# Score and key products of 64 rows, issued in alternating pairs of row halves

## The reference

```
s = jnp.einsum('bqhmd,bkhmd->bhmqk', qblk, k).astype(jnp.float32) * scale
p = jax.nn.softmax(s, axis=-1)
a = p[:, :, 0] - lam * p[:, :, 1]
return jnp.einsum('bhqk,bkhe->bqhe', a.astype(v.dtype), v)
```

```
kk = jnp.einsum('bhncd,bhnsd->bhncs', kc, kc)
a_mat = jnp.where(strict, bc[..., :, None] * kk * decay, 0.0) + jnp.eye(CHUNK, dtype=jnp.float32)
sol = lax.linalg.triangular_solve(a_mat, rhs, left_side=True, lower=True, unit_diagonal=True)
qk = jnp.where(incl, jnp.einsum('bhncd,bhnsd->bhncs', qc, kc) * decay, 0.0)
```

## Time and profile before

| | |
|---|---|
| median of three runs | 1831.31 us (1827.92 to 1831.51) |
| span of the profiled execution | 1824.8 us |
| time of the profiled execution | not listed apart from its span; the three runs lie 3.1 to 6.7 us above that span |
| PE busy | 1692.8 us, 93% of the span |
| DVE busy | 1013.0 us, 56% |
| ACT busy | 476.5 us, 26% |
| chain that ended last | PE 79%, DVE 15%, ACT 3%, issue 2% |
| attention's sixteen big units | 95.4 us (824.11 to 919.48) |
| make stage, one unit in the steady part | 20.0 us |

### The profile page before, as it was taken

The page is one execution under the profiler, slowest core; times in us unless marked ns, Lnnn a source line. Parts: engine busy times, 40 slices in busy tenths (PEclk is TensorE's granted clock), DMA queues, the critical chain, the costliest instruction groups (busy, mean ns, idle before and its releaser), DMA issues.

```text
span 1824.8 us, 28725 instructions
## 1 busy us (share of the span) xinstructions
PE 1692.8 (93%) x11299; PEld 1618.8 (89%) x11299; DVE 1013.0 (56%) x1765; ACT 476.5 (26%) x824; POOL 263.7 (14%) x213
## 2 busy tenths in 40 slices
PE   6799999999996999989878999888979999999997
PEld 5799999999996998866668888788979999999997
DVE  5766666664536764856647887678452332222223
ACT  4322222221213333324541110112232222221112
POOL 1200000000003000010026665663030000000000
PEclk9799999999997999996889999869979999999999
DMA  8344444453322221210000000000212222222221
GB/s 269 100 142 138 138 138 138 138 161 103 122 86 81 70 81 47 58 59 0 1 6 1 1 1 1 21 10 1 81 35 80 70 71 78 76 73 81 70 78 72
DMA packets 187755, 135.90 MB, mean 74 GB/s; under 512 B 8176, under 2 KB 173349, under 8 KB 187557
## 3 DMA queue, kind: packets, MB, share of 16 engines
q1 hardware_dynamic: 164981, 112.39, 20.4%
q10 hardware_dynamic: 22704, 22.55, 4.1%
HBM read 131.51 MB, written 3.41 MB: 74 GB/s over the span
## 4 chain that ended last, share of the span: by engine, by line
PE 79%; DVE 15%; ACT 3%; issue 2%; DMA 0%; POOL 0%; DVEq 0%; SPq 0%; ACTq 0%
PE ps L1341 20%; PE ps L1343 20%; PE ps L1342 20%; PE ps L1711 3%; PE ps L1715 2%; PE ps L1599 2%; PE ps L1388 1%; DVE h_lo L807 1%; PE ps L1757 1%; PE ps L1620 1%; PE ps L1691 1%; DVE r_s L1137 1%; DVE conv_acc L956 1%; DVE h_hi L806 1%; DVE att_s L1039 1%
## 5 line engine op out<-in xcount | busy, mean ns | idle before, releaser
L1341 PE MATMUL ps<-h_hi,w_lo 128*128 128x320 f32 x1920 | 607.1, 316 | 39.0 <-DVE h_lo L807 32.0
L1342 PE MATMUL ps<-h_lo,w_hi 128*128 128x320 f32 x1920 | 599.7, 312 | 0.0
L1343 PE MATMUL ps<-h_hi,w_hi 128*128 128x320 f32 x1920 | 599.5, 312 | 0.0
L777 DVE TENSOR_TENSOR w_lo<-w_raw,w_hi 128x1024 fp32r<-128x1024 f32 x168 | 206.1, 1228 | 391.1 <-ACT w_hi L483 389.6
L1341 PEld LDWEIGHTS ps<-h_hi,w_lo 128*128 128x128 f32 x1920 | 366.7, 191 | 46.4 <-issue 21.8
L1342 PEld LDWEIGHTS ps<-h_lo,w_hi 128*128 128x128 f32 x1920 | 367.1, 191 | 1.0 <-issue 0.7
L1343 PEld LDWEIGHTS ps<-h_hi,w_hi 128*128 128x128 f32 x1920 | 366.4, 191 | 0.0
L483 ACT CAST w_hi<-w_raw 128x1024 fp32r<-128x1024 f32 x168 | 175.4, 1045 | 290.6 <-PE ps L1343 227.6
L1341 PE MATMUL ps<-act_hi,w_lo 128*128 (+1 forms) x704 | 218.0, 310 | 0.0
L1343 PE MATMUL ps<-act_hi,w_hi 128*128 (+1 forms) x704 | 217.7, 309 | 0.0
L1342 PE MATMUL ps<-act_lo,w_hi 128*128 (+1 forms) x704 | 217.7, 309 | 0.0
(11 more groups left out here) (277 smaller groups left out, 2088.3 us busy)
## 6 DMA issues: line engine op xcount, KB each, us to landing
w_raw<-in_w_ffn_in SPq DMA_DIRECT2D x88, 512.0 KB, 3.9
w_raw<-in_w_ffn_out SPq DMA_DIRECT2D x44, 512.0 KB, 3.6
ada_ffn<-in_w_ada ACTq DMA_DIRECT2D x43, 512.0 KB, 3.7
w_raw<-in_w_in SPq DMA_DIRECT2D x28, 512.0 KB, 3.8
ada_ffn<-in_w_ada SPq DMA_DIRECT2D x13, 512.0 KB, 3.5
ada_tile<-in_w_ada SPq DMA_DIRECT2D x10, 512.0 KB, 7.7
w_raw<-in_w_out SPq DMA_DIRECT2D x8, 512.0 KB, 4.1
ada_wide<-in_w_ada SPq DMA_DIRECT2D x3, 1024.0 KB, 8.6
```

The costliest lines, as they stand in the source:

```text
L777: nc.vector.tensor_tensor(w_lo[s][:], w_raw[s][:], w_hi[s][:].bitcast(F32), ALU.subtract)\
L1341: nc.tensor.matmul(out, lo, xh, start=start, stop=False)
L1342: nc.tensor.matmul(out, hi, xl, start=False, stop=False)
L1343: return nc.tensor.matmul(out, hi, xh, start=False, stop=stop)
```

## The change

In attention, scores(v) now waits once, for both exponentials of the unit before, and issues its matmuls in alternating pairs: map 0 (rows 0 to 63) and map 1 (rows 64 to 127), first for one half of the keys, then for the other. In the make stage, the eight products of a unit are all issued at k = 3, in two calls that alternate between the row halves, each half into another bank; nothing is left at k = 2 and k = 4, and DVE's k = 5 waits for PE's sixth signal instead of its fourth. The number of matmuls and signals is the same.

```
                 if k == 5:
-                    dve.wait_ge(t_pe[c], pe0 + 4)
+                    dve.wait_ge(t_pe[c], pe0 + 6)
...
             def scores(v):
                 hb, q0, nk = ATT_UNITS[v]
-                for m in range(2):
-                    if v >= 1:
-                        pe.wait_ge(s_exp, 2 * v - 1 + m)
-                    rows = slice(m * DK, m * DK + DK)
-                    q = q_b[rows, hb, q0:q0 + P]
-                    if nk == P:
-                        ins = nc.tensor.matmul(ps[:, 2 * m, 0:P], q, k_b[rows, hb, 0:P], start=True, stop=True)
-                    else:
-                        for half in range(2):
-                            ins = nc.tensor.matmul(ps[:, 2 * m + half, 0:HT], q, k_all[rows, hb, half * HT:half * HT + HT],
-                                                   start=True, stop=True)
-                    ins.then_inc(s_mm, 1)
+                if v >= 1:
+                    pe.wait_ge(s_exp, 2 * v)
+                for half in range(1 if nk == P else 2):
+                    for m in range(2):
+                        rows = slice(m * DK, m * DK + DK)
+                        q = q_b[rows, hb, q0:q0 + P]
+                        if nk == P:
+                            out, keys = ps[:, 2 * m, 0:P], k_b[rows, hb, 0:P]
+                        else:
+                            out, keys = ps[:, 2 * m + half, 0:HT], k_all[rows, hb, half * HT:half * HT + HT]
+                        ins = nc.tensor.matmul(out, q, keys, start=True, stop=True)
+                        if half == 1 or nk == P:
+                            ins.then_inc(s_mm, 1)
...
-            def products(t, g, c, bank, which, e):
-
+            def products(t, g, c, bank, e):
                 for h in (e, e + 2):
-                    ins = nc.tensor.matmul(ps[:, bank, h * P:(h + 1) * P], qk(t, g, h, 4), qk(t, g, h, which),
-                                           start=True, stop=True)
-                ins.then_inc(t_pe[c], 1)
+                    for out, hh, which in ((bank, h, 4), (bank + 1, h + 1 - 2 * e, 0)):
+                        ins = nc.tensor.matmul(ps[:, out, hh * P:(hh + 1) * P], qk(t, g, hh, 4), qk(t, g, hh, which),
+                                               start=True, stop=True)
+                        if h == e + 2:
+                            ins.then_inc(t_pe[c], 1)
...
-                if k == 2:
-                    pe.wait_ge(t_dve[c], dve0 + 1)
-                    products(t, g, c, bank, 4, 0)
                 if k == 3:
-                    pe.wait_ge(t_pe[c], r * PE_T + 3)
-                    products(t, g, c, bank, 4, 1)
                     pe.wait_ge(t_dve[c], dve0 + 2)
-                    products(t, g, c, bank + 1, 0, 0)
-                if k == 4:
-                    pe.wait_ge(t_pe[c], r * PE_T + 5)
-                    products(t, g, c, bank + 1, 0, 1)
+                    products(t, g, c, bank, 0)
+                    pe.wait_ge(t_pe[c], r * PE_T + 4)
+                    products(t, g, c, bank, 1)
```

## The result

The changed kernel takes 1860.16 us in the median of four runs (1858.85 to 1861.20), against 1831.41 us before (1827.92 to 1832.90). The ratio is 1.0161, with a 95% interval of 1.0149 to 1.0174: slower by 28.8 us.

A forecast was written before the change was run, and what follows sets the result against it. It took attention's PE and DVE lists as both nearly full, kept so by staggered maps, and DVE as setting gaps in the make stage. Attention +19.0 and make stage +4.8 gave +23.8, hence 1855 us (1841 to 1869).

The forecast's parts named there:

- a ring in attention: Attention: scores, maximum, weights, maximum, exponential run one after another, 6.3 us per cycle at full clock, 7.3 at lower; +19.0 us.
- an outgrown gap in the make stage: Make stage: the k = 3 block takes 1.45 us instead of 0.68, 0.54 of the extra stays per steady unit; +4.8 us.
- The next three: Attention, three big-unit cycles behind the first, 16.75 us together: at the lower clock 3 x 7.3 us; +5.1 us.
- The three groups of three: Attention, nine later big-unit cycles, 48.57 us: 6.3 us each, a third of scores at lower clock; +10.8 us.
- Norm cycles: Attention, three cycles with norm work, already in serial order: a third of 0.94 us more each; +0.9 us.
- Small units: Attention, the small units' cycles lose their stagger too, 0.5 us each; +1.5 us (0 to 3).
- the clock rival: All attention scores at lower clock (+29), make stage's clock pulled down in places (+10); up to 1875 us, chance 0.15.
- Pairs worth nothing of their own: Attention and make stage: row halves already overlap where nothing holds them apart, so alternating order adds no overlap.
- PE as the bound: Rival: pairs free PE, three lower-clock attention cycles save 3 us, make stage 7; 1821 us, chance 0.04.
- The in-order rule: Skill's claim: matmuls keep program order in start and end, so only list neighbours overlap and alternating would gain.
- The change does nothing: Rival: attention's second exponential is mostly done anyway, cycles stay, make stage +-5 us; 1831 us, chance 0.03.
- The ring at full clock alone: Rival: attention loses 11 us with its steps serial at full clock, make stage gains 7; 1835 us, chance 0.09.

The follow-up runs named there:

- experiment 3: Kernel before, with attention's scores waiting once for the second exponential but keeping the order map 0, then map 1: 1855.18 us, ratio 1.0130.
- experiment 1: Kernel before with only the change's new attention scores (one wait, alternating pairs), make stage as before: 1854.54 us, ratio 1.0121.
- experiment 4: Kernel before with the change's new attention scores, and DVE's weights moved ahead of the maximum of map 0: 1822.23 us, ratio 0.9948.
- experiment 2: Kernel before with only the change's new product block in the make stage, attention as before: 1834.56 us, ratio 1.0023.
- experiment 5: Kernel before, scores unchanged with two waits, only DVE's weights moved ahead of the maximum of map 0: 1820.15 us, ratio 0.9933.
- experiment 6: Kernel before with one wait for the scores in map order, and DVE's weights ahead of the maximum of map 0: 1822.44 us, ratio 0.9948.
- experiment 7: Kernel before, attention unchanged, make stage's products in two alternating groups at k = 3 and k = 4: 1832.47 us, ratio 1.0008.
- experiment 8: Kernel before, attention unchanged, make stage's products in two alternating groups at k = 2 and k = 3: 1828.45 us, ratio 0.9981.
- experiment 9: Kernel before, attention unchanged, all eight products at k = 3, even and odd heads in separate banks, no wait inside: 1833.62 us, ratio 1.0019.

## Why the prediction was right

I said 1855 us (1841 to 1869) by a ring in attention and an outgrown gap in the make stage; measured 1860.16.

**Attention.** The mechanism was right: experiment 3 makes the loss of experiment 1 by the wait alone, and experiment 4 takes it away by DVE's order alone. The sizes by groups: first cycle +0.7, measured 5.71 to 6.42, +0.7. The next three +5.1, measured 16.75 to 21.65, +4.9. The three groups of three +10.8, measured 48.57 to 60.8, +12.2. Two errors partly cancel here, which is luck. The ring took 6.06 us at full clock, and I had taken 6.3: the cycle of the earlier trace rows that I read as one at full clock began at the lower one,

```profile
889.44:890.00 0.56, 0.56 (x3) 0.46 (x4) 0.03 (x1) 0.35 (x1) 0.00 (x0) 0.50 0.00 0
```

with the first half of a microsecond of its scores. Nine cycles were 2.2 us too long by that. But six of the nine, and not a third, had scores at the lower clock for some or all of their length (they took 6.5 to 7.2 us): 6.2 us over 9 x 6.06, where I had 2.7.

Norm cycles +0.9, measured +1.5. Small units +1.5, measured +2.4: they lose 0.8 each, not 0.5. Together 19.0 forecast and 21.7 measured.

**Make stage.** The block: 1.45 us forecast, 1.46 measured. The period: 20.5 forecast, 20.55 measured, and the hole at k = 4, put at 0.5, is 0.35. The six periods from the first of the seven steady blocks to the last grew by 3.3 us. But the stage grew by 9.1 us in the profile, and I had +4.8. The stretch before these periods and the one behind them are 2.9 us each longer, with 20.2 us at the lower clock in the stage instead of 9.0. I had put 1.0 into the first of them (second and third unit) and one block's 0.54 into the last.

The last stretch in experiment 2, which has the same block, and then in the changed kernel:

```profile
1117.90:1165.15 47.25, 38.81 (x309) 34.45 (x309) 30.88 (x48) 1.28 (x2) 20.23 (x16) 1.00 0.00 1
1140.17:1190.42 50.25, 41.80 (x306) 37.08 (x306) 30.83 (x48) 1.28 (x2) 20.24 (x16) 0.90 0.00 1
```

In the kernel before this stretch takes 47.31 us (1111.10 to 1158.41). So at full clock the seventh block costs nothing there, and the 2.9 us come with the clock. That is the loss that the clock rival speaks of, in a place that I hadn't named: not in the steady part, where the granted clock stayed 1.00, but before and behind it. That the block pulled the clock down isn't shown. In experiments 1, 3, 4, 5 and 6 the make stage is that of the kernel before, and in their profiles it takes 218.2 to 225.3 us, with 6.8 to 23.9 us at the lower clock. The longest is that of experiment 5:

```profile
926.47:1151.73 225.26, 199.79 (x1530) 180.67 (x1529) 159.80 (x290) 33.63 (x95) 128.19 (x101) 0.95 0.01 2
```

Experiment 2 puts the part at 3.5 to 4.2 us by its runs, so over many executions the 4.8 was near; its one profile has 7.1.

I put 0.2 us to the changes of row mode. That is what a whole block takes beyond its matmuls, going in and coming back, so that four changes fewer are 0.4 us and not 0.8. What part of it is the change of mode no run separates. No term hung on it.

**Pairs worth nothing of their own.** Right, and shown apart by experiments 3 and 6.

**The rivals.** PE as the bound is out by experiments 1, 2 and 7. The in-order rule fell with experiment 3. "The change does nothing" is out. The make stage gains only in the form of experiment 8, where the blocks fit the gaps. The ring at full clock alone (1835 us) is out by the measured time.

**Where the 5 us to the forecast lie:** 2.7 in attention (small units, clock), 0.9 between the stages and 4.3 in the make stage, nearly all in its two ends. That is by the one profiled execution of each kernel, whose difference of 32.3 us is itself 3.5 above that of the medians.

## What to carry to other kernels

That an engine is full doesn't mean that sparing it work pays: before merging two waits or moving a small block, look at what stands between them on the other engines. Here PE's small blocks in the make stage lay in gaps that DVE set. In attention the single wait cost some 23 us by the lost stagger, and the 8.6 us less that PE was busy in the big units bought nothing.

When a merged wait closes a ring, look for an operation on the other engine that depends only on the same event, and put it first: DVE's weights ahead of the maximum turned 6.06 us into 4.66. The same move in the kernel before, without any change on PE, made it 0.7% faster (experiment 5).

Price a block that is moved by the gap at its new place, not by the time it takes: blocks of 1.46, 1.10 and 0.64 to 0.68 us at k = 3 gave periods of 20.55, 20.18 and 19.78 to 20.00.

## What the hardware showed

Float32 matmuls on the two row halves overlap even when one half's instructions all stand before the other's in the list: in the make stage before, eight records in 0.72 us as against four in 0.71; in attention, eight records in 1.35 us at full clock and 2.5 at the lower one in either order (experiments 1 and 3). Sixteen records of both halves, in alternating order, took 1.16 us (experiment 9).

A wait of PE for its own matmuls of the other half left the weight loads idle for 0.29 us, and cost 0.37 us of the period (20.55 against 20.18, experiments 2 and 9).

The granted clock didn't follow PE's busy share. Over attention's big units it was 0.78 with PE busy 89% of the time (before), 0.74 with 66% (after), 0.89 with 71% (experiment 4) and 0.85 with 88% (experiment 5). In the three cycles from 829.82 on PE was busy all the time, and the granted clock was 0.53, that is 1.2 GHz for nearly all of it. What sets it these runs don't tell.
